# Triangular inverse of RWKV-7 chunks: diagonal blocks of 16 rows on 128 partitions, joined in pairs by PE, in place of blocks of 32 rows by columns

## The reference, cut to what matters

```python
def step(state, inp):
    r_t, k_t, v_t, w_t, kk_t, b_t = inp
    sa = jnp.einsum('bhvk,bhk->bhv', state, -kk_t)
    state = (state * w_t[:, :, None, :] + sa[..., None] * b_t[:, :, None, :]
             + v_t[..., None] * k_t[:, :, None, :])
    return state, jnp.einsum('bhvk,bhk->bhv', state, r_t)
```

## Time and profile before

| what | us |
|---|---|
| median of 3 runs | 1381.35 |
| lowest and highest | 1379.21, 1381.46 |
| the profiled execution, its own time | 1384.91 |
| its span in the trace | 1383.1 |
| mean granted TensorE clock, as a share | 0.805 |

### The profile page before, as it was taken

The page is one execution under the profiler, slowest core; times in us unless marked ns, Lnnn a source line. Parts: engine busy times, 40 slices in busy tenths (PEclk is TensorE's granted clock), DMA queues, the critical chain, the costliest instruction groups (busy, mean ns, idle before and its releaser), DMA issues. The chain is left out here.

```text
span 1383.1 us, 15924 instructions
## 1 busy us (share of the span) xinstructions
PE 1004.3 (73%) x6111; PEld 616.2 (45%) x6111; DVE 616.1 (45%) x1276; ACT 303.9 (22%) x517; POOL 99.3 (7%) x82
## 2 busy tenths in 40 slices
PE   1699988985686778768675699605978888788820
PEld 1355555663565646667663345502323333343310
DVE  2318997455666776877424233260111111111125
ACT  2320000416153352732115311001100010011001
POOL 0000000010000101001000000041111111011131
PEclk9799999998665757556577798756999999999975
DMA  9825421110001111011409011145999999665543
GB/s 339 301 105 228 159 78 56 31 23 9 10 22 16 24 16 24 1 17 24 155 12 365 40 46 46 46 185 192 409 419 420 419 415 416 246 235 204 209 140 137
DMA packets 81415, 215.79 MB, mean 156 GB/s; under 512 B 48406, under 2 KB 48784, under 8 KB 64448
## 3 DMA queue, kind: packets, MB, share of 16 engines
q1 hardware_dynamic: 71040, 196.13, 37.7%
q0 software_dynamic: 7520, 10.63, 2.2%
q10 hardware_dynamic: 2783, 8.06, 1.6%
HBM read 206.96 MB, written 22.51 MB: 166 GB/s over the span
## 5 line engine op out<-in xcount | busy, mean ns | idle before, releaser
L522 PE MATMUL bank<-arena 128*128 128x320 f32 x704 | 200.7, 445 | 14.3 <-DVE arena L414 6.1
L522 PEld LDWEIGHTS bank<-arena 128*128 128x128 f32 x704 | 135.3, 194 | 81.4 <-issue 29.9
L1968 PE MATMUL bank<-arena 128*64 128x512 f32 x512 | 128.8, 661 | 29.4 <-DMA arena<-in_expert_w_up 28.4
L922 DVE SCALAR_TENSOR_TENSOR arena<-arena 128x655 f32<-128x655 f32 x116 | 104.6, 902 | 4.6 <-DVE arena L922 0.2
L1968 PEld LDWEIGHTS bank<-arena 128*64 128x64 f32 x512 | 44.3, 152 | 113.1 <-issue 111.7
L1449 PE MATMUL bank<-arena 128*128 128x512 f32 x160 | 78.7, 655 | 11.6 <-issue 11.6
L2049 DVE TENSOR_TENSOR arena<-arena,bank 128x256 f32<-128x256 f32 x16 | 6.7, 422 | 154.7 <-ACT arena L2023 154.7
L1885 PE MATMUL bank<-arena 128*128 128x512 f32 x128 | 61.9, 640 | 12.9 <-DMA arena<-in_expert_w_up 7.2
L1990 PE MATMUL bank<-arena 128*64 128x512 f32 x256 | 60.2, 613 | 9.8 <-DVE arena L2052 9.8
L884 ACT ACTIVATE arena<-bank 64x128 f32<-64x128 f32 (+1 forms) x68 | 19.9, 292 | 171.6 <-PE bank L1257 170.3
L1449 PEld LDWEIGHTS bank<-arena 128*128 128x128 f32 x160 | 33.4, 212 | 54.2 <-issue 54.2
(11 more groups left out here) (287 smaller groups left out, 1527.4 us busy)
## 6 DMA issues: line engine op xcount, KB each, us to landing
arena<-in_expert_w_gate SPq DMA_DIRECT2D x40, 1024.0 KB, 16.3
arena<-in_expert_w_up SPq DMA_DIRECT2D x40, 1024.0 KB, 22.3
arena<-in_expert_w_down SPq DMA_DIRECT2D x40, 1024.0 KB, 20.3
arena<-in_ada_w SPq DMA_DIRECT2D x12, 2048.0 KB, 10.2
arena<-in_w_in SPq DMA_DIRECT2D x22, 512.0 KB, 3.6
arena<-expert_rows SPq DMA_DIRECT2D x10, 512.0 KB, 8.4
arena<-in_x_sample SPq DMA_DIRECT2D x8, 512.0 KB, 7.6
arena<-in_w_out SPq DMA_DIRECT2D x1, 4096.0 KB, 14.8
```

The lines of the kernel that those rows point to most:

```text
L522: mm = nc.tensor.matmul(psum[4 + 2 * (n % 2) + half][:, 0:HALF], wring[:, n % NWIN, k], hT[:, k, half * HALF:(half + 1) * HALF], start=(k ...
L922: chain(nc.vector.scalar_tensor_tensor(acc, src, w, acc, ALU.mult, ALU.add))
L1968: mm = nc.tensor.matmul(psum[2 + n % 2][r, :], xeT[:, n % 2, c, r], gu[:, :, c, :], start=(c == 0), stop=(c == KD - 1))
```

## The change

The diagonal blocks are now of 16 rows. Each matrix has four, so the 32 matrices of a unit give 128 blocks, one a partition, and each block is inverted once. DVE goes through 15 rows t, then writes a turned copy of the result (`WIT`). SP stores both (`winv`, `winvt`) and loads eight pieces: for each pair of blocks the turned upper inverse (`WT`) and the lower one (`WLOW`), and the four inverses straight into the diagonal blocks of GM, without ACT. The store of the blocks of U takes four DMAs instead of two, its load one instead of two. New events pair_y and pair_z on PE join two blocks of 16 to one of 32, 64 matmuls of 16x16 as stated in each event (32 matrices, two pairs), in turn on partitions 0 to 15 and 32 to 47; ACT copies the results out, two copies each. place, merge_y and merge_z follow as before, but place no longer starts with ACT's two copies. The places of the new events are in the diff. In ACT's order they come to stand before T6 (0.795) and behind it (0.805), in PE's before S6 (0.840) and behind it (0.875).

```diff
@@ -154,9 +154,9 @@
         KN = CS
         inva, invb = regr.take(COLS), regr.take(COLS)
-        UL = inva.rearrange("p (s t) -> p s t", t=32)
-        WI, WTMP = (x.rearrange("p (s j) -> p s j", j=16) for x in (invb[:, 0:512], invb[:, 512:1024]))
-        WB = invb.rearrange("p (n q j) -> p n q j", q=2, j=16)
+        UL, WIT = (x.rearrange("p (s t) -> p s t", t=16) for x in (inva[:, 0:256], inva[:, 256:512]))
+        WI, WTMP = (x.rearrange("p (s j) -> p s j", j=16) for x in (invb[:, 0:256], invb[:, 256:512]))
+        WT, WLOW, YP = (x.rearrange("p (n j) -> p n j", j=16) for x in (inva[:, 512:1024], invb[:, 512:1024], invb[:, 0:512]))
         TA = Y1 = inva.rearrange("p (n t) -> p n t", t=32)
         def unit_set():
@@ -552,8 +552,8 @@
         gateb, gsig = view(zbase + 3 * PAIRS * ZT + ZT, DR), view(zbase + 3 * PAIRS * ZT + ZT + DR, T)
         s_wout, s_gateb = sem("w_out_landed"), sem("gate_lora_landed")
-        udiag = dram("udiag", [5, 64, 1024])
-        winv = dram("winv", [5, 2, 64, 512])
+        udiag = dram("udiag", [5, P, 256])
+        winv, winvt = dram("winv", [5, P, 256]), dram("winvt", [5, P, 256])
         cout = dram("conv_out", [4, P, CT])
         UNITS = [[(d, j, ZS, TS, (j - j0) * TS) for j in (j0, j0 + 1)] for d in range(2) for j0 in (0, 2)]
@@ -592,7 +592,7 @@
         EARLY = ["shift_r", "shift_k", "shift_v", "lora_w", "lora_a", "square", "scan", "norm", "exp", "kn", "kp"]
         FILL = ["ar", "bk", "gram0", "gram1", "gram2", "gram3", "invload", "bonus", "scale", "turn_bk", "turn_v", "mv"]
-        INVERT = ["inv0", "inv1", "inv2", "inv3", "inv4", "invstore", "place", "merge_y", "merge_z"]
+        INVERT = ["inv0", "inv1", "inv2", "inv3", "inv4", "invstore", "pair_y", "pair_z", "place", "merge_y", "merge_z"]
         CHAIN = ["X", "T", "S", "Y"]
         ENGINES = ("pe", "act", "dve", "sp", "pool")
         Z_PLACES = [-3.2 + 0.1 * n for n in range(16)] + [-1.40, -1.2, -1.0, -0.73, -0.68, -0.62]
@@ -615,7 +615,9 @@
             "inv2": (0.566, 0.593, 0.383, 0.537, 0.518),
             "inv3": (0.626, 0.597, 0.534, 0.724, 0.649),
             "inv4": (0.646, 0.602, 0.707, 0.739, 0.736),
-            "invstore": (0.688, 0.701, 0.782, 0.889, 0.748),
+            "invstore": (0.688, 0.701, 0.782, 0.800, 0.748),
+            "pair_y": (0.840, 0.795, 0.800, 0.900, 0.860),
+            "pair_z": (0.875, 0.805, 0.802, 0.910, 0.865),
             "place": (0.923, 0.815, 0.808, 0.976, 0.879),
             "merge_y": (0.961, 0.886, 0.925, 1.053, 0.979),
             "merge_z": (1.014, 0.937, 0.987, 1.060, 0.991),
@@ -671,7 +673,7 @@
                 "gram2": [("g4", 0), ("g5", 1)], "gram3": [("g6", 2), ("g7", 3)],
                 "bonus": [("b0", 2), ("b1", 3)], "turn_bk": [(f"t{q}", q) for q in range(4)],
                 "turn_v": [(f"v{q}", q) for q in range(4)], "mv": [(f"m{q}", q) for q in range(4)],
-                "place": [("ta0", 0), ("ta1", 1)], "merge_y": [("y0", 2), ("y1", 3)],
+                "pair_y": [("p0", 2)], "pair_z": [("q0", 3)], "place": [("ta0", 0), ("ta1", 1)], "merge_y": [("y0", 2), ("y1", 3)],
                 "merge_z": [("z0", 0), ("z1", 1)]}
         BANK = {use: bank for uses in USES.values() for use, bank in uses}
         FILLED, READ = {}, {}
@@ -706,7 +708,6 @@
         s_ar, s_bk, s_bkh = sem("ar_ready"), sem("bk_ready"), sem("bk_scaled")
         s_ud, s_ul, s_wd, s_wb = sem("udiag_stored"), sem("udiag_loaded"), sem("winv_stored"), sem("winv_loaded")
         s_inv = sem("inverse_done")
-        s_wcopy = sem("inverse_blocks_placed")
         s_sl, s_slT, s_s0 = sem("states_loaded"), sem("states_turned"), sem("initial_states_ready")
         s_X, s_XS, s_SA, s_SAS = sem("x_summed"), sem("x_taken"), sem("removals_summed"), sem("removals_taken")
         s_S, s_ST, s_Y, s_YS = sem("state_summed"), sem("state_ready"), sem("y_summed"), sem("y_added")
@@ -732,28 +733,32 @@
                     wait_read(sp, u, "g7")
                     for r in range(3):
                         wait_read(sp, u, f"g{4 + r}")
-                    for b in range(2):
-                        sp.dma_start(udiag[u, 32 * b:32 * b + 32].rearrange("n (s t) -> s n t", t=32),
-                                     GM[u % 2][32 * b:32 * b + 32, :, 32 * b:32 * b + 32]).then_inc(s_ud, 16)
+                    for b in range(4):
+                        r = slice(16 * b, 16 * b + 16)
+                        sp.dma_start(udiag[u, 32 * b:32 * b + 32].rearrange("n (s t) -> s n t", t=16),
+                                     GM[u % 2][r, :, r]).then_inc(s_ud, 16)
                 elif ev == "invload":
-                    sp.wait_ge(s_ud, 32 * (u + 1))
+                    sp.wait_ge(s_ud, 64 * (u + 1))
                     if u:
                         wait_read(sp, u - 1, "z0")
                         wait_read(sp, u - 1, "z1")
-                    for q in range(2):
-                        sp.dma_start(UL[64 * q:64 * q + 64].rearrange("p s t -> p (s t)"), udiag[u]
-                                     ).then_inc(s_ul, 16)
+                    sp.dma_start(UL.rearrange("p s t -> p (s t)"), udiag[u]).then_inc(s_ul, 16)
                 elif ev == "invstore":
                     sp.wait_ge(s_inv, u + 1)
-                    sp.dma_start(winv[u].rearrange("q n f -> (q n) f"), WI.rearrange("p s j -> p (s j)")
-                                 ).then_inc(s_wd, 16)
-                    sp.wait_ge(s_wd, 16 * (u + 1))
-                    for b in range(2):
-                        for q in range(2):
-                            sp.dma_start(WB[32 * b:32 * b + 32, :, q, :],
-                                         winv[u, q, 32 * b:32 * b + 32].rearrange("n (s j) -> s n j", j=16)
-                                         ).then_inc(s_wb, 16)
+                    sp.dma_start(winv[u], WI.rearrange("p s j -> p (s j)")).then_inc(s_wd, 16)
+                    sp.dma_start(winvt[u], WIT.rearrange("p s j -> p (s j)")).then_inc(s_wd, 16)
+                    sp.wait_ge(s_wd, 32 * (u + 1))
+                    for b in (0, 2):
+                        sp.dma_start(WT[16 * b:16 * b + 16],
+                                     winvt[u, 32 * b:32 * b + 32].rearrange("n (s j) -> s n j", j=16)).then_inc(s_wb, 16)
+                        sp.dma_start(WLOW[16 * b:16 * b + 16],
+                                     winv[u, 32 * b + 32:32 * b + 64].rearrange("n (s j) -> s n j", j=16)
+                                     ).then_inc(s_wb, 16)
+                    for b in range(4):
+                        r = slice(16 * b, 16 * b + 16)
+                        sp.dma_start(GM[u % 2][r, :, r],
+                                     winv[u, 32 * b:32 * b + 32].rearrange("n (s j) -> s n j", j=16)).then_inc(s_wb, 16)
                 elif ev == "final":
                     for use in ("la0", "la1"):
                         wait_read(sp, u, use)
@@ -855,14 +860,18 @@
                         else:
                             ins_ = nc.scalar.activation(SAV[b][64:128, 4 * q:4 * q + 4, :], src[64:128], ACT.Copy)
                         chain.announce(ins_, s_read[BANK[f"{name}{q}"]], read_count(u, f"{name}{q}"))
+                elif ev in ("pair_y", "pair_z"):
+                    use = "p0" if ev == "pair_y" else "q0"
+                    wait_filled(act, u, use)
+                    for k in range(2):
+                        r = slice(32 * k, 32 * k + 16)
+                        dst = YP[r] if ev == "pair_y" else GM[b][r, :, 32 * k + 16:32 * k + 32]
+                        ins_ = nc.scalar.activation(dst, psum[BANK[use]][r, :].rearrange("p (n j) -> p n j", j=16), ACT.Copy)
+                        if k == 0:
+                            chain(ins_)
+                    chain.announce(ins_, s_read[BANK[use]], read_count(u, use))
                 elif ev == "place":
-                    act.wait_ge(s_wb, 64 * (u + 1))
-                    for k in range(2):
-                        r = slice(32 * k, 32 * k + 32)
-                        chain.announce(nc.scalar.activation(
-                            GM[b][r, :, 32 * k:32 * k + 32].rearrange("p n (j q) -> p n j q", q=2),
-                            WB[r].rearrange("p n q j -> p n j q"), ACT.Copy), s_wcopy, 2 * u + k + 1)
                     for h in range(2):
                         wait_filled(act, u, f"ta{h}")
                         chain.announce(nc.scalar.activation(
@@ -1041,26 +1050,19 @@
                 elif ev.startswith("inv") and ev[3:].isdigit():
                     part = int(ev[3:])
                     if part == 0:
-                        dve.wait_ge(s_ul, 32 * (u + 1))
-                        if u:
-                            dve.wait_ge(s_wcopy, 2 * u)
-
-                        chain(nc.vector.memset(invb[:, 0:512], 0.0))
-                        for q in range(2):
-                            chain(nc.vector.memset(invb[64 * q:64 * q + 64, 16 * q:512:33], 1.0))
-                    cuts = [31, 26, 20, 14, 7, 0]
```

(37 more changed lines are left out.)

## The result

The changed kernel takes 1390.11 us (median of 20 runs, 1382.40 to 1395.95), the kernel before in the same session 1380.64 (20 runs, 1376.40 to 1385.19): a ratio of 1.0063 with an interval of 1.0049 to 1.0078, or +8.7 us (the two medians lie 9.5 apart). The profiled execution of after has its own time of 1395.38 and a span of 1393.6, 10.5 us over the span before; it lies 5.3 above the median of after, as the one before lay 3.6 above its own.

A forecast was written before the change was run, and what follows sets the result against it. No engine was taken as full; the wait ending last in each slot bounds it: DVE and PE nearly level, then latency from store to place. Slots +5.95 twice, +4.65, +3.65, unit 0 +8.3: +28.5, 1410 us, range 1397 to 1441.

The forecast's parts named there:

- Part (b): Between landing and place, pair_y and pair_z replace ACT's two 1.30 us copies: 30 ns a record, 3.9 us a stage.
- the term from ready to place: From all loads landed to place: later by 9.55 us in each slot, 8.3 for unit 0, +46.5 in all.
- Rival B: Pair products on PE: a 16x16 record costs no less than a 32x32, 54 ns, 7.0 us a stage; 1441 us; chance 0.25.
- Part (a): Store to landing, with two stores and eight loads: 8.5 us instead of 6.8, +1.7 a unit, bounds +0.5 to +4.1.
- rival C: Dear DMAs: eight loads keep 0.57 to 0.75 us of issue each, or 16 partitions land slower; 1414 to 1422; chance 0.10.
- How much earlier the inverse ends: End of the inverse earlier by 5.3 us in slots 0 and 1, 6.6 in slot 2, 7.6 in slot 3, 1.7 for unit 0.
- A: Faster, since DVE bounds the preparation: the whole 12.8 us comes off each unit, -9 us, 1372; chance 0.07.

The follow-up runs named there:

- x5: Kernel before with the inverse's loop over t cut to its last 15 rows, 30 DVE operations instead of 62 a unit: ratio 0.9664, stage 17.5 us shorter.
- x4: Changed kernel with the two loops of pair_y and pair_z exchanged, 32 matmuls in a row on one tile instead of alternating: ratio 1.0155.
- x7: Kernel before with its four loads of the inverse cut into eight of 16 partitions: ratio 1.0058, all loads landed 8.77 us after the store.
- x16: x7 with two loops exchanged, so loads to the same 16 partitions follow each other: one execution, 1397.03 us beside 1383.76.
- x17: Changed kernel with its eight loads reordered so that no two to the same 16 partitions are issued one behind the other: ratio 1.0048.
- x9: Changed kernel with the rows of winv and winvt 2 KB apart in DRAM instead of 1 KB: ratio 1.0062.
- x10: Changed kernel with the pair join later in the order, pairs waiting for four loads alone, and winv and winvt rows 2 KB apart: ratio 0.9983.
- x12: Changed kernel with the four loads into GM issued ahead of the four into WT and WLOW: ratio 1.0065.
- x3: Changed kernel with GM's four loads on their own semaphore, for which place waits; pair_y waits for the first four loads alone: ratio 1.0015.

## Why the prediction was wrong in size

**Direction, mechanism and places: right.** The inverse is shorter by what was said, its store goes out earlier, and the time is lost again between the store and place, with T6 and S6 behind pair_y. x5 shows that DVE's relief is worth 17.5 us in the stage; the table has the whole of both sides, 37.1 of gain and 48.8 of cost.

**Part (b), the price of a pair record: wrong, -20 us.** The prediction had "By size alone a record would be 27 ns; I take 30". The 27 came from place, which runs on one tile, and it is exact for one tile (27.4 in x4). The same paragraph had seen that alternation halves X's and Y's price, said that pair alternates as well, and then did not halve. It is 14.8 ns; a pair event takes 1.9 us instead of 3.9, twice in each of five units. The lower bound, 23 ns, was too high for the same reason. With 1.9 us the term from ready to place would have been 26.5 us instead of 46.5, and 28.6 were measured.

**Rival B: refuted.** No record of 16x16 takes its 54 ns. The Trainium skill, "TensorEngine Tiling (Array Packing)", section "Instruction Overhead", was cited for it with some 60 cycles a matmul, an estimate of 50 ns at 1.2 GHz. Taken for a matmul as the program states it, which is two records, x4 has 54.8 ns and the alternating form 29.5: it may hold on one tile, and does not across two. The prediction had set it against the record.

**Part (a), store to ready: wrong, +10.9 us.** "+1.7" was right for what it counted (x7: +1.8). The bound of +4.1, set for dear issues, holds the measured +3.9, but in four of five units an issue took 0.49 us and was not the cause; in slot 2 alone one issue took 2.13. What the runs show in its place: the order of the loads has a part (1.07 us in x16, 0.5 to 0.8 in x17), the packets end 1.3 us later and the landing comes 0.8 later still behind them, and the cause of 1.3 us or more stays open. It is rival C's size by another cause; "16 partitions land slower than 32" was named there, and x7 shows that this is not it either.

**How much earlier the inverse ends: wrong, -10.6 us.** For slot 1 the 5.3 was right (5.7 measured); there mv ran at the lower level, as in all four slots before. In slots 0 and 3 it ran at the upper one, where the prediction had taken its 6.7 us over from before. The windows ahead of mv say what PE did: before, from 388.0,

```profile
388.00:392.40 4.40, 0.69 (x8) 0.51 (x8) 3.32 (x15) 3.10 (x5) 0.00 (x0) 0.64 0.00 0
```

and after, ahead of mv and during it:

```profile
386.00:392.20 6.20, 5.93 (x73) 5.16 (x72) 3.15 (x13) 4.79 (x10) 0.00 (x0) 1.00 0.16 31
393.20:400.00 6.80, 6.80 (x106) 5.57 (x104) 4.93 (x17) 6.45 (x12) 0.00 (x0) 1.00 0.00 0
...
472.00:480.00 8.00, 7.90 (x86) 7.78 (x88) 3.02 (x14) 5.50 (x10) 0.00 (x0) 0.54 0.01 2
```

Before, PE stood nearly idle there, since the chain waited for DVE and DVE for the blocks, and the granted clock came down from 1.00 to 0.50 in this window, ahead of mv. After, with the shorter round trip (6.0 us instead of 8.9), PE is busy 5.93 of 6.2 us, the clock stays at 1.00, and mv takes 3.72 us. The last row is mv in slot 1, at the lower level again, though the round trip is short there too (6.95 us) and PE had been busy for 5.08 of the 6.70 us before it, at 1.00. So the short round trip goes with the upper level, but doesn't settle it. In slot 2 it ran at the upper level (3.78 us) and the inverse still gained only 4.3 of the predicted 6.6, so there another step was too high; which of them was not tried.

**The clock across the runs.** Over the fifteen profiled executions of the changed kernel and its variants, the time from inv0 to the store in slot 0 is 24.1 to 24.5 us in twelve and 29.1 to 29.8 in three (x9, x10, x12); in the twelve mv takes 3.9 us from first to last record, in the three 5.2 to 5.9. In slot 1 it is 23.4 to 24.7 in five, with mv at 3.9, and 29.2 to 31.0 in ten, with mv at 5.3 to 7.1. Nothing lies between. A slot is thus worth some 5 to 7 us by the level that mv and the matmuls behind it get, and it can differ from one execution to the next: the 13.6 us between the fastest and slowest run of the changed kernel are of the size of two slots, though unprofiled runs don't show their slots. In x5, which relieves DVE but keeps the long round trip of the blocks, mv took 7.1 us in all four slots. In x7 and x16, with the long round trip too, it took 6.6 to 7.1. So it is the round trip, and not the steps of DVE, that goes with the clock; that it is the cause was not tried by changing the round trip alone.

**The chances.** A, DVE as bound, was refused rightly for these slots: what inv1 to inv3 save did become DVE's idle time in slot 1, 4.54 us ahead of its addition of S3 as forecast (4 to 5), though only 1.35 in slot 0, where mv was fast:

```profile
480.01 0.29 DVE L1109 TENSOR_TENSOR arena<-bank,arena 128x128 f32<-128x128 f32 x1 [4.54 <-PE bank L1284]
```

The chance of 0.04 for "within 0.2%" and 0.07 for faster went with the direction, and the range should have reached down: with the halving that the rows of X and Y gave, and a pair event at the 1.9 us measured, the sum is +8.5 and the forecast 1390. That this would have met the measured time is luck: the two other errors, +10.9 and -10.6, nearly cancel.

## What to carry to other kernels

Price a small matmul first on one tile, by size, and then for alternation between tiles: here the two factors, a half each, multiplied. Shortening an engine's work pays only where it ends last, but a shorter wait can leave PE without a gap, and here what followed then ran at the other clock in most executions; look at PE's idle stretches ahead of the big blocks of matmuls before and after a change. When a transfer is on the path, wait for the part that is needed first (x3: half a per cent) before anything is said of its place in the order.

## What the runs showed of the hardware that was not expected

A 16x16 float32 record on alternating tiles costs 14.8 ns at granted clock 0.50, 27.4 on one tile. The Trainium skill's page "TensorE: Matmul & The Clock Gate", before the section "Seeing it yourself", has about 25 ns from start to start as a floor; a record is under it, a stated matmul (29.5) is not. Packets of 64 bytes were under way for 10 ns each or for 68, for the same count and bytes, in eight loads of another order and destination; with two loads to the same 16 partitions issued one behind the other (x16 beside x7), ready came 1.07 us later. The landing of the last load followed its last packet by 1.2 us in the mean in x7, 2.0 in the changed kernel and 2.3 in x12.
